# Products without a use between the first conditioning units, first norm's squares added by VectorE, down projections begun two tiles early

## The chip, the cores and the metric

One core of a Trainium2 chip runs the whole program. The metric is the device time of one execution in microseconds (us), lower is better. TensorE does the matrix products, VectorE (DVE) and ScalarE (ACT) take results out of PSUM and split operands, GpSimd (POOL) does additions beside them, and SyncE (SP) issues nearly all loads. TensorE's granted clock has two levels, 1.2 and 2.4 GHz; the profile gives it as a share of 2.4 (0.50 and 1.00).

## The reference, cut to what matters

Two blocks run one after the other on 256 tokens of width 1024 (the first block also carries 256 context tokens). All arrays are float32. What the change touches:

```python
# conditioning of a layer: 6 vectors of 1024 for each of two token sets
mod_l = (silu(c) @ w_ada + b_ada)          # w_ada: 1024 x 6144
hl = rms_norm(xl, norm_mix) * (1 + sc1_l) + sh1_l     # the first norm

# rms_norm: x * rsqrt(mean(x * x) + 1e-6) * g

# the feed-forward parts, four in all (two per block), D_FF = 2816 = 22 x 128
swiglu(h) = (silu(h @ w_g) * (h @ w_u)) @ w_d

# second block, a chunked recurrence with gates: its 64 x 64 systems
# are solved level by level; the gates are products h @ w_gate, sigmoid
```

## The kernel before, in words

**Operands.** Activations lie feature-major: 128 features on the partitions, tokens along the row. Each float32 product is made of three faster ones: weights and activations are split into a high and a low part, and `weight_tile` (L639) issues high x high, high x low and low x high. ScalarE writes the high part of a weight unit (`act_split`, L603, L612), VectorE the low part (`dve_split`, L615, L621), both ahead of TensorE by two units. A unit is at most 128 x 2048 elements, 1 MB. SyncE loads units in the order of the list UNITS into a ring of three slots (`load_unit`, L547); a slot is free when the unit that lay there is split, or, for the conditioning weights ("raw" units), multiplied (`raw_done`).

**The start.** Eight raw units hold the first 2048 columns of the conditioning weights. `pe_ada` (L1008) goes through them on TensorE: for unit x the products `ada_products` (L989: eight products of 256 columns, each with 32 stationary columns, float32, in four column groups), then the fold of unit x - 1 (`ada_fold`, L1000, four records for two products of 2 columns), which needs ScalarE's copy of that unit (`take_ada`, L1006). A unit's products also wait until the copy of the unit two before is done. Between the units stand the sums of squares of the first norm. `act_ada` (L1026) is ScalarE's side: before the copies of units 3 to 6 it squares two tiles of 128x512 each (L727) into three buffers in turn; TensorE adds each square over the partitions by a product with a matrix of ones (`pe_square_sum`, L750), which also frees its buffer. Before the copy of unit 7 ScalarE loads the table of the square root with a small root of its own (L762) and takes the root of the sum (L767). VectorE then forms the reciprocal (L781), waits for the last fold (`ada_cols`), adds the bias to the conditioning columns (L1106), forms the scales (L1109) and scales the tokens (L802), with the low parts (L794) and two weight splits between. TensorE's first product of tokens is L647. SyncE issues in this order: parameters, raw unit 0, common constants, x (2 MB, L3077), raw units 1 to 7, and then the units of the projections.

**A feed-forward part.** `pe_ffn` (L895) goes through the up tiles: for tile i the gate and up products; ScalarE applies silu (L945), VectorE multiplies (L970), writes the high part (L972) and the low part (L973) of hidden tile i and counts `h_gated`. Then it waits for all hidden tiles, and `pe_residual` (L651) runs the down projection: eight output groups m, each over all f hidden tiles k in order, one PSUM bank per group. The first feed-forward works on 512 tokens in two halves of f = 11 (phases down0_0 and down0_1), the other three on 256 tokens with f = 22: five down projections in all. In the first one GpSimd forms part of the second layer's conditioning beside it (L1080 to L1084), summed by TensorE (L1094).

**The recurrence.** `pe_rwkv` (L2458) runs four groups, each with a solve over levels (`pe_level_p`, L2351; `pe_level_u`, L2367 and L2369), values (L2380, copied by ScalarE, L2542), the solved systems (`pe_solved`, L2391 without and L2397 with the values) and a scan of four steps that begins when ScalarE has copied the solution (L2546, L2548). Into the waits between these TensorE fits pieces of the gate product (`pe_gate`, L2828: one piece is three products of 256 columns).

Of the kernel before, what the change touches and what calls it, by code (L numbers as in the profile page):

```python
# [8 lines left out]
ALU = mybir.AluOpType  # L9
# [3 lines left out]
P = 128  # L13
D = 1024
KT = D // P
# [20 lines left out]
RING = 3  # L36
# [379 lines left out]
ADDS = KT - 2  # L416
SUMS_DONE = [KT + sum(x is not None for x in SUMS[1:r + 1]) for r in range(len(SUMS))]

# [13 lines left out]
def build(nc, dram, out):  # L432
    ctx = ExitStack()
    with ctx:
# [68 lines left out]
        def K(name):  # L503
            at, n = CONST_AT[name]
            return const[:, at:at + n]
# [144 lines left out]

        def pe_residual(pe, phase, h, c0, n, kt, norm=None, order=None, first=0):  # L651


            s0, g0 = FIRST_OF_KIND[phase], FIRST_GROUP[phase]
            order = order or list(range(kt))
            for m in range(KT):
                bank = GROUPS[g0 + m][0] if first and m < 2 else pe_group(pe, g0 + m)
                for x, k in enumerate(order):
                    if first and m < 2 and x < kt - first:
                        continue  # L660
                    t = m * kt + x
                    if t % TPU == 0:
                        pe_weights(pe, s0 + t // TPU)
                    mm = weight_tile(pe, ps[:, bank, 0:n], s0 + t // TPU, t % TPU * P, P, h[:, k, 0, c0:c0 + n],
                                     h[:, k, 1, c0:c0 + n], x == 0, x == kt - 1)
                    if x == kt - 1:
                        mm.then_inc(group_done, 1)
                    elif t % TPU == TPU - 1:
                        mm.then_inc(unit_done, 1)
            if norm is not None and norm not in LATE:  # L670
                pe_square_sums(pe, norm)
# [44 lines left out]
        def act_square(act, r, m):  # L716
# [3 lines left out]
            if r and m == 0:  # L720
                act.wait_ge(norm_sum, SUMS_DONE[r - 1])
            elif m >= 3 and r == 0:
                act.wait_ge(norm_sum, m - 2)
            elif m >= 3:
                act.wait_ge(norm_add, ADDS * (SUMS[r] - 1) + m - 2)
# [6 lines left out]
        def square_at(r, m):  # L732
            return m % 3 if r == 0 else 0 if m == 0 else 1 + (m - 1) % 2

# [11 lines left out]

        def pe_square_sum(pe, m):

            pe.wait_ge(norm_sq, m + 1)
            pe.matmul(ps[:, 5, :], K("ones"), square[:, square_at(0, m), :], start=(m == 0), stop=(m == KT - 1)).then_inc(norm_sum, 1)  # L750

# [143 lines left out]
        def pe_ffn(pe, r, norm, next_norm):  # L895
            hidden, h, n, c0 = ffn_operands(r)
            for x, f in enumerate(FFN_PARTS[r]):
# [21 lines left out]
                if r == 0 and x == len(FFN_PARTS[0]) - 1:  # L919
                    pe_ada_fold(pe, ADA_UNITS + ADA_FIRST - 1)  # L920
                pe.wait_ge(h_gated, hidden_done(r, x, f))
                final = x == len(FFN_PARTS[r]) - 1
                pe_residual(pe, f"down{r}_{x}", hidden, 0, n, f, next_norm if final else None)

# [57 lines left out]

        FIRST_SUMS = 3

# [18 lines left out]
        def take_ada(act, x, bank):  # L1003

            act.wait_ge(raw_done, x + 1)
            act.activation(ada_row(x), ps[:, bank, 0:ADA_COLS], ACT.Copy).then_inc(ada_rows, 1)  # L1006

        def pe_ada(pe):  # L1008
            pe.wait_ge(cond_ready, 2)
            for x in range(ADA_FIRST + 1):  # L1010
                if x < ADA_FIRST:
# [5 lines left out]
                else:  # L1017
                    pe.wait_ge(ada_rows, x)
                    mm = ada_fold(pe, x - 1, x - 1)
                    if x == ADA_FIRST:  # L1020
                        mm.then_inc(ada_cols, 1)
                if FIRST_SUMS <= x < FIRST_SUMS + KT // 2:
                    for m in range(2):
                        pe_square_sum(pe, 2 * (x - FIRST_SUMS) + m)

        def act_ada(act):  # L1026
            for x in range(ADA_FIRST):
                if x == FIRST_SUMS:
                    act.wait_ge(x_in, 16)
                if FIRST_SUMS <= x < FIRST_SUMS + KT // 2:  # L1030
                    for m in range(2):
                        act_square(act, 0, 2 * (x - FIRST_SUMS) + m)
                if x == ADA_FIRST - 1:
                    act_root_ready(act)
                    act_root(act, 0)
                take_ada(act, x, 4 + 2 * (x % 2))
# [1421 lines left out]
        def pe_rwkv(pe):  # L2458
            for g in range(RW_GROUPS):
# [23 lines left out]
                pe_level_p(pe, g, 4)  # L2483
                pe_gate(pe, 2 * g + 1, 5, 7)
                pe_level_u(pe, g, 4)
                pe_values(pe, g)
                pe_solved(pe, g)
                pe_gate(pe, 2 * g + 1, 7, 10)
                for c in range(4):
# [527 lines left out]
        def _(dve):  # L3017
# [3 lines left out]
            dve.memset(eps_col[:, 3:4], EPS * EPS)  # L3021
            dve.memset(cond[:, :, 2:32], 0.0).then_inc(cond_ready, 1)
            for layer in range(DEPTH):
                c0, n = unit_tokens(layer, False)
# [48 lines left out]
        def _(sp):  # L3073
            sp.dma_start(par[:, :], dram["par"]).then_inc(par_in, 16)
            load_unit(sp, 0)
            sp.dma_start(const[:, 0:COMMON_N], dram["const"][:, 0:COMMON_N]).then_inc(const_in, 16)
            sp.dma_start(xT[:, :, :].rearrange("p k t -> p (k t)"), dram["x"]).then_inc(x_in, 16)  # L3077
            for u in range(1, len(UNITS)):
                if u == RAW_UNITS[ADA_FIRST - 1] + 4:
                    sp.dma_start(const[:, COMMON_N:COMMON_N + ONE_N], dram["const"][:, COMMON_N:COMMON_N + ONE_N]).then_inc(first_in, 16)  # L3080
# [121 lines left out]
```

## Time and profile before

| | us |
|---|---|
| median of 3 runs (lowest, highest) | 1990.88 (1985.06, 1994.65) |
| the profiled execution | 1997.22 |
| its span, first to last instruction | 1995.4 |
| TensorE busy | 1859.6 (93%) |
| VectorE, ScalarE, GpSimd busy | 1155.0, 769.7, 300.9 |

The mean granted clock of the profiled execution is 0.969. Busy shares overlap; what sets the time is read from the chain of waits, which follows the last instruction back to what released it. In a timeline a row gives start, duration, engine, line, operation and operands, and in brackets the idle time before it with what ended it. Durations of pipelined products overlap, so the distance of two starts says more than a duration. A float32 product leaves two records, so x4 at L750 is two products.

### The profile page before, as it was taken

How to read it: one execution, taken by the hardware profiler on the slowest of the kernel's cores; microseconds unless marked ns; L12 is line 12 of the kernel's file. 1: busy time of each engine (PE TensorE's matmuls, PEld its weight loads, DVE VectorE, ACT ScalarE, POOL GpSimd, SP SyncE). 2: the span in 40 equal slices, each digit the busy share in tenths (PEclk: the TensorE clock that was granted, in tenths of full speed). 3: DMA queues.
4: the chain of work that ended last, by engine and by line, in shares of the span. 5: the costliest groups of instructions: out<-in, count | busy, mean ns of one | idle time of the engine just before them, and what ended most of it. 6: DMA issues, size and time to landing. Idle time of an engine off the chain costs nothing.

```text
span 1995.4 us, 34393 instructions
## 1 busy us (share of the span) xinstructions
PE 1859.6 (93%) x14988; PEld 1636.1 (82%) x14988; DVE 1155.0 (58%) x1708; ACT 769.7 (39%) x1073; POOL 300.9 (15%) x264
## 2 busy tenths in 40 slices
PE   6999878999999998887999999999998999999998
PEld 3777556777888777766999999999988778899997
DVE  2744574655253327656655576555668777676654
ACT  3432562321122224455433443333454444344332
POOL 0011001799262010100000100002001111000000
PEclk9998989999999998899999999999999999999999
DMA  8254113466354212203455565553431111255552
GB/s 322 84 195 164 64 34 115 149 196 203 116 164 153 95 65 74 96 1 127 148 177 173 180 204 185 176 183 127 159 138 44 44 44 66 86 169 188 175 174 77
DMA packets 40758, 266.22 MB, mean 133 GB/s; under 512 B 4512, under 2 KB 4640, under 8 KB 13344
## 3 DMA queue, kind: packets, MB, share of 16 engines
q1 hardware_dynamic: 35712, 244.10, 35.4%
q0 software_dynamic: 4608, 16.78, 2.7%
q8 instruction: 118, 1.93, 0.4%
q10 hardware_dynamic: 288, 3.15, 0.4%
q14 instruction: 32, 0.26, 0.0%
HBM read 262.96 MB, written 1.05 MB: 132 GB/s over the span
## 4 chain that ended last, share of the span: by engine, by line
PE 76%; DVE 13%; ACT 5%; POOL 4%; issue 2%; DMA 1%; SPq 0%; ACTq 0%; DVEq 0%; POOLq 0%
PE ps L641 19%; PE ps L642 18%; PE ps L643 18%; DVE W L621 3%; PE ps L1620 2%; POOL work L1080 2%; PE ps L989 2%; ACT W L612 1%; POOL work L1081 1%; PE ps L647 1%; PE ps L1407 1%; PE ps L2351 1%; PE ps L649 1%; PE ps L648 1%; PE ps L2369 1%
## 5 line engine op out<-in xcount | busy, mean ns | idle before, releaser
L621 DVE TENSOR_TENSOR W<-ring,W 128x2048 fp32r<-128x2048 f32 (+2 forms) x194 | 442.8, 2284 | 257.1 <-ACT W L612 256.8
L612 ACT ACTIVATE W<-ring 128x2048 fp32r<-128x2048 f32 (+2 forms) x194 | 359.0, 1853 | 139.7 <-PE ps L643 130.6
L641 PE MATMUL ps<-h_lat,W 128*128 128x256 f32 x1056 | 302.0, 286 | 5.8 <-DVE h_lat L794 4.0
L642 PE MATMUL ps<-h_lat,W 128*128 128x256 f32 x1056 | 299.9, 284 | 0.0
L643 PE MATMUL ps<-h_lat,W 128*128 128x256 f32 x1056 | 299.9, 284 | 0.0
L641 PEld LDWEIGHTS ps<-h_lat,W 128*128 128x128 f32 x1056 | 203.6, 193 | 7.5 <-issue 4.6
L642 PEld LDWEIGHTS ps<-h_lat,W 128*128 128x128 f32 x1056 | 203.9, 193 | 0.3 <-issue 0.2
L643 PEld LDWEIGHTS ps<-h_lat,W 128*128 128x128 f32 x1056 | 203.8, 193 | 0.0
L745 POOL TENSOR_TENSOR work<-work 128x256 f32<-128x256 f32 (+1 forms) x42 | 41.0, 977 | 972.9 <-ACT work L727 781.8
L641 PE MATMUL ps<-hidden_lat,W 128*128 128x256 f32 x528 | 151.1, 286 | 6.3 <-DVE hidden_lat L973 6.3
L642 PE MATMUL ps<-hidden_lat,W 128*128 128x256 f32 x528 | 150.7, 286 | 0.0
L643 PE MATMUL ps<-hidden_lat,W 128*128 128x256 f32 x528 | 150.7, 285 | 0.0
L970 DVE TENSOR_TENSOR work<-work,ps 128x256 f32<-128x256 f32 (+1 forms) x88 | 42.9, 488 | 185.8 <-ACT work L945 185.7
L641 PE MATMUL ps<-h_both,W 128*128 128x512 f32 x352 | 140.7, 400 | 8.9 <-DVE h_both L794 8.9
L642 PE MATMUL ps<-h_both,W 128*128 128x512 f32 x352 | 137.8, 391 | 0.0
L643 PE MATMUL ps<-h_both,W 128*128 128x512 f32 x352 | 137.7, 391 | 0.0
L945 ACT ACTIVATE work<-ps 128x512 f32<-128x512 f32 (+1 forms) x44 | 21.6, 490 | 267.7 <-PE ps L643 267.7
L641 PEld LDWEIGHTS ps<-hidden_lat,W 128*128 128x128 f32 x528 | 102.8, 195 | 6.9 <-DVE hidden_lat L973 6.9
L643 PEld LDWEIGHTS ps<-hidden_lat,W 128*128 128x128 f32 x528 | 102.7, 195 | 0.0
L642 PEld LDWEIGHTS ps<-hidden_lat,W 128*128 128x128 f32 x528 | 102.7, 195 | 0.0
L727 ACT ACTIVATE work<-xT 128x256 f32<-128x256 f32 (+1 forms) x64 | 31.6, 496 | 172.3 <-DVE xT L688 112.4
L641 PE MATMUL ps<-h_mix,W 128*128 128x256 f32 x312 | 92.7, 297 | 5.2 <-DVE h_mix L792 3.9
(402 smaller groups left out, 4315.4 us busy)
## 6 DMA issues: line engine op xcount, KB each, us to landing
ring<-w_up_dram SPq DMA_DIRECT2D x88, 1024.0 KB, 4.9
ring<-w_down_dram SPq DMA_DIRECT2D x43, 1024.0 KB, 4.9
ring<-w_ada_dram SPq DMA_DIRECT2D x32, 1024.0 KB, 5.6
work<-w_ada_dram POOLq DMA_DIRECT2D x32, 512.0 KB, 4.1
ring<-w_rkv_dram SPq DMA_DIRECT2D x13, 1024.0 KB, 4.9
ring<-w_fm_dram SPq DMA_DIRECT2D x10, 1024.0 KB, 4.9
ring<-w_out_dram SPq DMA_DIRECT2D x8, 1024.0 KB, 4.8
ring<-w_gates_dram SPq DMA_DIRECT2D x16, 512.0 KB, 3.6
```

The lines of the kernel that those rows point to most:

```text
L612: act.activation(slots[SLOT[s]][:, 0, 0:cols], ring[:, u % RING, 0:cols], ACT.Copy).then_inc(w_high, 1)
L621: dve.tensor_tensor(slots[SLOT[s]][:, 1, 0:cols], ring[:, u % RING, 0:cols], slots[SLOT[s]][:, 0, 0:cols], ALU.subtract).then_inc(w_low, 1)
L641: pe.matmul(o, slots[SLOT[s]][:, 0, at:at + cols], high, start=first, stop=False)
L642: pe.matmul(o, slots[SLOT[s]][:, 0, at:at + cols], low, start=False, stop=False)
L643: return pe.matmul(o, slots[SLOT[s]][:, 1, at:at + cols], high, start=False, stop=final)
L727: ins = act.activation(square[:, at, 0:n], xT[:, m, c0:c0 + n], ACT.Square, scale=1.0 / 32)
L745: pool.tensor_tensor(square[:, 0, 0:n], square[:, 0, 0:n], square[:, square_at(r, m), 0:n], ALU.add).then_inc(norm_add, 1)
L945: act.activation(stage_buf[:, i % 2, 0:n], gate, ACT.Silu).then_inc(act_emptied, 1)
L970: dve.tensor_tensor(t, t, up_banks(g, n)[1], ALU.mult).then_inc(dve_emptied, 1)
L989: mm = pe.matmul(ps[32 * g:32 * g + 32, bank, 0:ADA_COLS], cond[:, k, :], w[:, k * ADA_COLS:(k + 1) * ADA_COLS], start=(k < 4), stop=(k >= ...
L1080: plink(pool.tensor_tensor(half, half, c, ALU.mult))
L1620: mm = pe.matmul(ps[:, 2 + d, 65 * tt:65 * tt + 65], pbuf[:, s, d, tt * P:(tt + 1) * P], vones[:, s, h, :], start=(s == src[0]), stop=(s = ...
```

## The change

Four edits.

1. Start, order of loads: x is issued behind raw unit 2, just before raw unit 3. ScalarE squares four tiles before the copy of unit 3 and four before the copy of unit 4, loads the root's table there too, and takes the root before the copy of unit 6. The squares use the buffers of the later norms (one that holds the sum, two in turn).
2. Start, sums: VectorE adds the squares into one tile (seven additions of 128x512), and TensorE makes one sum over the partitions, after unit 5. The counts for the later norms (`SUMS_DONE`) fall from 8 to 1 for the first norm.
3. Start, products without a use: `pe_warm` issues float32 products of the conditioning vector's tile with itself (128 stationary columns, 256 moving) into a bank that nobody reads: 3 before unit 0, then 1 after each unit but the last, and 9 after unit 2.
4. Down projections wait at first for f - 2 hidden tiles, and for all of them before tile f - 2 of the first group. And in the recurrence one of the two gate pieces ahead of the last level's update, and one of the three behind the solve, move between the values and the solve.

```diff
-SUMS_DONE = [KT + sum(x is not None for x in SUMS[1:r + 1]) for r in range(len(SUMS))]
+SUMS_DONE = [sum(x is not None for x in SUMS[:r + 1]) for r in range(len(SUMS))]
...
-        def pe_residual(pe, phase, h, c0, n, kt, norm=None, order=None, first=0):
+        def pe_residual(pe, phase, h, c0, n, kt, norm=None, order=None, first=0, late=None):
...
+                    if late is not None and (m, k) == (0, late[0]):
+                        pe.wait_ge(*late[1:])
...
-                act.wait_ge(norm_sum, m - 2)
+                act.wait_ge(first_add, m - 2)
...
-            return m % 3 if r == 0 else 0 if m == 0 else 1 + (m - 1) % 2
+            return 0 if m == 0 else 1 + (m - 1) % 2
...
-        def pe_square_sum(pe, m):
-
-            pe.wait_ge(norm_sq, m + 1)
-            pe.matmul(ps[:, 5, :], K("ones"), square[:, square_at(0, m), :], start=(m == 0), stop=(m == KT - 1)).then_inc(norm_sum, 1)
+        first_add = sem("first_add")
+
+        def dve_first_sums(dve):
+
+            for m in range(1, KT):
+                dve.wait_ge(norm_sq, m + 1)
+                if m >= 2:
+                    dve.wait_ge(first_add, m - 1)
+                dve.tensor_tensor(square[:, 0, :], square[:, 0, :], square[:, square_at(0, m), :], ALU.add).then_inc(first_add, 1)
+
+        def pe_first_sum(pe):
+
+            pe.wait_ge(first_add, KT - 1)
+            pe.matmul(ps[:, 5, :], K("ones"), square[:, 0, :], start=True, stop=True).then_inc(norm_sum, 1)
...
-                pe.wait_ge(h_gated, hidden_done(r, x, f))
+                pe.wait_ge(h_gated, hidden_done(r, x, f - 2))
                 final = x == len(FFN_PARTS[r]) - 1
-                pe_residual(pe, f"down{r}_{x}", hidden, 0, n, f, next_norm if final else None)
+                pe_residual(pe, f"down{r}_{x}", hidden, 0, n, f, next_norm if final else None,
+                            late=(f - 2, h_gated, hidden_done(r, x, f)))
...
-        FIRST_SUMS = 3
+        FIRST_SUM = 5
...
+        def pe_warm(pe, n):
+
+            for _ in range(n):
+                pe.matmul(ps[:, 0, 0:COND_N], const[:, cond_at:cond_at + P], const[:, cond_at:cond_at + COND_N], start=True, stop=True)
+
         def pe_ada(pe):
             pe.wait_ge(cond_ready, 2)
+            pe_warm(pe, 3)
...
-                if FIRST_SUMS <= x < FIRST_SUMS + KT // 2:
-                    for m in range(2):
-                        pe_square_sum(pe, 2 * (x - FIRST_SUMS) + m)
+                if x < ADA_FIRST - 1:
+                    pe_warm(pe, 9 if x == RING - 1 else 1)
+                if x == FIRST_SUM:
+                    pe_first_sum(pe)
 
         def act_ada(act):
             for x in range(ADA_FIRST):
-                if x == FIRST_SUMS:
+                if x == RING:
                     act.wait_ge(x_in, 16)
-                if FIRST_SUMS <= x < FIRST_SUMS + KT // 2:
-                    for m in range(2):
-                        act_square(act, 0, 2 * (x - FIRST_SUMS) + m)
-                if x == ADA_FIRST - 1:
+                for m in {RING: range(4), RING + 1: range(4, KT)}.get(x, ()):
+                    act_square(act, 0, m)
+                if x == RING + 1:
                     act_root_ready(act)
+                if x == FIRST_SUM + 1:
                     act_root(act, 0)
                 take_ada(act, x, 4 + 2 * (x % 2))
...
-                pe_gate(pe, 2 * g + 1, 5, 7)
+                pe_gate(pe, 2 * g + 1, 5, 6)
                 pe_level_u(pe, g, 4)
                 pe_values(pe, g)
+                pe_gate(pe, 2 * g + 1, 6, 8)
                 pe_solved(pe, g)
-                pe_gate(pe, 2 * g + 1, 7, 10)
+                pe_gate(pe, 2 * g + 1, 8, 10)
...
             dve.memset(cond[:, :, 2:32], 0.0).then_inc(cond_ready, 1)
+            dve_first_sums(dve)
...
-            sp.dma_start(xT[:, :, :].rearrange("p k t -> p (k t)"), dram["x"]).then_inc(x_in, 16)
             for u in range(1, len(UNITS)):
+                if u == RING:
+                    sp.dma_start(xT[:, :, :].rearrange("p k t -> p (k t)"), dram["x"]).then_inc(x_in, 16)
```

## Rows read from the trace of the kernel before

**Rows 1.** The page, chain that ended last: share of the span by engine.
```profile
PE 76%; DVE 13%; ACT 5%; POOL 4%; issue 2%; DMA 1%; SPq 0%; ACTq 0%; DVEq 0%; POOLq 0%
```
**Rows 2.** Timeline of TensorE, start: start us, duration, engine, line, operation, [idle before].
```profile
14.26 1.93 PE L989 MATMUL ps<-ring,const 128*32 128x256 f32 x16 [5.94 <-DMA ring<-w_ada_dram]
16.12 1.01 PE L1000 MATMUL ps<-const,work 128*128 128x2 f32 x4
...
22.61 3.76 PE L750 MATMUL ps<-work,const 128*128 128x512 f32 x4
...
28.74 1.96 PE L750 MATMUL ps<-work,const 128*128 128x512 f32 x4
...
37.35 1.07 PE L989 MATMUL ps<-ring,const 128*32 128x256 f32 x16
38.35 1.18 PE L1000 MATMUL ps<-const,work 128*128 128x2 f32 x8
45.02 0.56 PE L647 MATMUL ps<-W,h_in 128*128 128x272 f32 x1 [5.49 <-DVE h_in L794]
```
**Rows 3.** Timelines of ScalarE and VectorE, start.
```profile
3.75 0.22 ACT L2986 ACTIVATE const<-par 128x16 f32<-128x16 f32 x1 [1.72 <-DMA par<-par_dram]
...
19.34 1.14 ACT L727 ACTIVATE work<-xT 128x512 f32<-128x512 f32 x2
...
35.53 1.28 ACT L762 ACT_TABLE_LOAD   x1
...
37.46 0.69 ACT L767 ACTIVATE work<-ps,eps_col 128x512 f32<-128x512 f32 x1 [0.43 <-PE ps L750]
38.18 3.35 DVE L781 RECIPROCAL work<-work 128x512 f32<-128x512 f32 x1 [36.97 <-ACT work L767]
...
41.57 0.19 DVE L1106 TENSOR_TENSOR mod<-ps,par 128x32 f32<-128x32 f32 x1
```
**Rows 4.** DMA in 3 to 9 us.
```profile
DMA packets 378, 2.52 MB, mean 420 GB/s; under 512 B 41, under 2 KB 169, under 8 KB 177
```
**Rows 5.** Timeline of TensorE, first product of each of the five down projections.
```profile
489.94 0.80 PE L641 MATMUL ps<-hidden_both,W 128*128 128x512 f32 x1 [3.54 <-DVE hidden_both L973]
...
684.58 0.50 PE L641 MATMUL ps<-hidden_both,W 128*128 128x512 f32 x1 [2.25 <-DVE hidden_both L973]
...
1082.47 0.39 PE L641 MATMUL ps<-hidden_lat,W 128*128 128x256 f32 x1 [1.72 <-DVE hidden_lat L973]
...
1278.38 0.39 PE L641 MATMUL ps<-hidden_lat,W 128*128 128x256 f32 x1 [2.29 <-DVE hidden_lat L973]
...
1919.69 0.58 PE L641 MATMUL ps<-hidden_lat,W 128*128 128x256 f32 x1 [2.29 <-DVE hidden_lat L973]
```
**Rows 6.** Windows: stretch, length, PE, PEld, DVE, ACT, POOL busy (xcount), granted clock, DMA, GB/s.
```profile
15.00:20.00 5.00, 5.00 (x40) 2.80 (x36) 0.00 (x0) 1.32 (x4) 0.00 (x0) 1.00 1.01 419
489.94:496.00 6.06, 6.06 (x14) 4.79 (x15) 2.68 (x1) 0.00 (x0) 5.58 (x5) 0.50 0.53 155
685.00:690.00 5.00, 5.00 (x24) 4.12 (x23) 1.74 (x1) 0.00 (x0) 0.00 (x0) 1.00 0.34 105
1083.10:1086.50 3.40, 3.40 (x18) 3.40 (x18) 2.20 (x1) 0.00 (x0) 0.00 (x0) 0.51 0.36 92
1087.00:1089.00 2.00, 2.00 (x19) 2.00 (x19) 0.00 (x0) 0.00 (x0) 0.00 (x0) 1.00 0.90 365
1919.69:1922.75 3.06, 3.06 (x14) 3.06 (x15) 2.29 (x1) 0.50 (x1) 0.00 (x0) 0.50 0.39 161
```
**Rows 7.** Timeline of VectorE ahead of the second down projection.
```profile
682.65 0.69 DVE L970 TENSOR_TENSOR work<-work,ps 128x512 f32<-128x512 f32 x1 [6.78 <-ACT work L945]
```
**Rows 8.** Timeline of TensorE, end of the first group's solve.
```profile
1551.33 0.39 PE L2838 MATMUL ps<-h_mix,gates_parts 128*128 128x256 f32 x1
...
1552.23 1.15 PE L2369 MATMUL ps<-work 64*64 64x64 f32 x32
...
1555.01 1.15 PE L2397 MATMUL ps<-work 64*64 64x64 f32 x32 [0.23 <-ACT work L2542]
```

## The prediction

> **What bounds the kernel now.** I read the page's shares first (TensorE is busy 93% of the span, in the table above), then its chain of waits, of which TensorE carries 76% [rows 1], so only idle or slow time of TensorE, or time before it can start, is worth anything. The view of waits then gives the places. At the start, TensorE is fed by eight conditioning units, interleaved with the sums of squares; the timeline of TensorE there [rows 2] shows the second unit only at 14.26 us, since the 2.1 MB of x stand ahead of it in the queue, and the last fold at 39.53 (38.35 and 1.18). ScalarE's and VectorE's rows [rows 3] show what follows one another: the root at 37.46, the reciprocal 38.18 to 41.53, and at 41.57 the addition that opens the first norm's scaling. That row is the mark for the start: all behind it up to the first token product at 45.02 is a chain of VectorE, then of splits. The other places are the starts of the five down projections: TensorE stands still until the last hidden tile's low part is written [rows 5], and in three of the five the granted clock is at its lower level, 1.2 GHz (0.50 in the rows), when it resumes or soon after [rows 6]. The solve of the recurrence has a small wait of 0.23 us in each of its four groups [rows 8].
>
> **The start.** Prices from rows 2. The eight products of a unit take 1.93 us at the low clock and 1.07 at the high one (I count 1.0 between starts), a fold 0.94 and 0.54 (half of 1.18 at the end, for two folds). Four records of square sums, two products of 512 columns, take 3.76 or 1.96. A product of no use has 256 columns and the same 128 rows, so a quarter of that: 0.94 or 0.49. There are 18: 3 ahead, 9 behind the third unit, 1 behind six others. The profile's granted clock says 1.00 in 15 to 20 us [rows 6], where the durations are those of the low level; they halve between the square sums at 22.61 and those at 28.74. For this stretch I go by durations.
>
> DMA moves 0.42 MB/us without a pause [rows 4]. A unit is 1.05 MB, 2.5 us. With x (5.0 us) out of its way the second unit lands at 9.2 instead of 14.2, the third at 11.7, x at 16.7, the others at 19.2, 21.7, 24.2, 26.7, 29.2, since each slot is freed in time. TensorE at the high clock by then: third unit ends by 13, nine products of no use reach 17.5, and the fourth unit runs from 19.2 to 20.2, as soon as it lands.
>
> ScalarE squares four tiles from 16.7. A square is 0.57 to 0.62 (1.14 for two [rows 3]); the trace has no addition of two 128x512 tiles in this stretch, so I bound it: 0.69 from the nearest row of VectorE, which reads PSUM too [rows 7], above, and half of it below; I take 0.69 plus 0.05 of hand-off. Then copy of the fourth unit to 20.8, four squares held by the two buffers to 23.5, table load and dummy root 1.5 [rows 3], copy of the fifth unit at 25.4. Here is a new wait: TensorE has the sixth unit's products done at 25.2 and cannot fold the fifth until 25.5, because ScalarE's copy stands behind the squares and the table load; queued behind the fold on TensorE are the square sum and the last two units. Then fold 26.1, product of no use 26.6, one square sum of 0.98 to 27.6 (VectorE's seventh addition is done by 24.3), root to 28.4, reciprocal 3.35 to 31.8. Beside it TensorE: seventh unit 28.6, fold 29.2, product 29.7, eighth unit 30.7, two folds 31.9. So the mark falls at 31.9, not 41.57: minus 9.7 us. The reciprocal and the conditioning end together, so neither alone is worth more. What comes behind keeps its offsets: the weights of the first projection wait on the sixth and seventh unit's products, which move more than that, and so do the constants.
>
> At the low clock throughout until the nine products raise it (around 20), the fourth unit runs at 22.2 to 23.3 and is copied at 23.7, ScalarE's second batch and the table load end at 27.7, the square sum at 30.2, the reciprocal at 34.4, and the mark is 34.6, minus 7.0. If the clock rises and then falls once more between 17.5 and 24, where TensorE is busy about half the time, the last four units and the square sum run at the low prices and the mark is near 36.5, minus 5. If all of it is low, the nine end at 24.2, the square sum at 37.3, the eighth unit at 42.9 and the folds at 44.7: mark 44.8, plus 3.2.
>
> The Trainium skill (TensorE: Matmul & The Clock Gate, "What's actually happening") says the throttled state is the default and activity releases it. By that the unbroken products from 14.26 should have raised the clock soon, and products of no use would be needless; the rows show the products of 14.26 and the square sums of 22.61 both at the low prices. By the page the units are fast from the start, the sum above is the same 9.7; by the rows it needs the dense products, and 7.0 is as fair.
>
> **The down projections.** Each issues all but the last two k-tiles of its first group before the new wait. That is 9 tiles x 3 products for the two parts of 11 tiles, 20 x 3 for the others. The rows at full clock show 24 products of 512 columns in 5.00 us, 0.21 each, and 19 of 256 columns in 2.00, 0.105 each [rows 6]; both count one product cut by each edge, so 0.23 and 0.12 are nearer. That is 5.6 to 6.2 and 6.3 to 7.2 us of work, against 1.72 to 3.54 us of waiting [rows 5]; the third tile from the end was written more than a whole up unit (48 products, 5 us or more) earlier. So the wait is wholly covered and all five gaps go: 3.54 + 2.25 + 1.72 + 2.29 + 2.29 = 12.1 us. The first weights are split two units ahead, and the bank was emptied two up units ago: neither is late next. Queued behind the moved wait is only the same group. A gap that goes takes its slow stretch with it. At 0.50 TensorE has 14 products of 512 columns in 6.06 us, which at 0.23 are worth 3.2; 18 of 256 columns in 3.40 us, some 16 of them whole, worth 1.9 to 2.0; and 14 in 3.06, worth 1.7 [rows 6]. Lost: 2.8 + 1.4 + 1.4 = 5.6 us. Together 17.7 us. None of it should be given back: weight splits here wait for TensorE to free slots, GpSimd's half of the later conditioning starts anew from TensorE's own step, and the projection's end is TensorE's.
> Bounds: all of it, or, if splits rather than TensorE set the pace of the first group, only the slow stretches.
>
> **The pieces of gate product in the solve.** One piece (three products; two take 0.90, from 1551.33 to 1552.23 [rows 8]) less before the last level's update, two after the values, two instead of three before the scan. Gain at best: the four waits of 0.23 go, 0.9 us. But the two pieces now stand ahead of the solve, whose result ScalarE must copy before the scan begins: update 0.4 earlier, then 0.8 of pieces, the copy's wait of 0.23 gone, so the scan starts about 0.24 later, four times: plus 1.0. I take the loss, since the scan already starts as the copy ends.
>
> **Sum**, against the profiled execution (1997.22, of which the span is 1995.4 and 1.8 lies around it): 9.7 + 17.7 - 1.0 = 26.4, to 1970.8. It lies 6.3 over the median of the three runs, 1990.88; how often a gap meets a slow stretch is the profile's luck, three of five here, and I have no reason to think the median had fewer. So I take the same 26.4 from the median: 1964.5, forecast 1965.
>
> **The rivals.**
> *The start's clock.* Same downs, but the start gains 5 to 7 (low until the nine products, or a second fall). Time 1967 to 1970. For it: the low prices from 14.26 to beyond 22.61 [rows 2], half-busy TensorE after 17.5. Against it: the dense stretch from 4.0 (conditioning vector ready at 3.97 [rows 3]) through the first unit and on into the second, all dense. Chance 30%.
> *Down gaps turn into another wait.* The unit's split, the bank, or the last tile comes late, and the five gaps are given back within the projection; only the start and part of the slow stretches stay: 9.7 + 3 - 1 = 11.7, 1979, or 1982 if no slow stretch goes either. Against it: VectorE is idle for 6.78 us before the last tile's product of the second part [rows 7], so nothing of its own is late. 8%.
> *The change doesn't do what it says at the start*: the mark is held by ScalarE (squares, table load, copies in one queue) so that both batches and the root come as late as now, gain 0 to 3, downs as forecast: 1971 to 1974. 7%.
> *Slower.* One mechanism: the products of no use run at 1.2 GHz, do not raise the clock, and TensorE stays low behind them. Place: the start and the projections behind it. Price: 3.2 us at the mark and 0.45 us for each us of product-bound work that follows low (1.4 of 3.06 [rows 6]). It decides only if it outlasts the 12.1 us of gaps and the 10 us of the bound below, some (12.1 + 10 - 3.2) / 0.45 = 42 us of low clock (rows 6 show stretches of 3 to 6). At 60 us of it the time is 1990.9 + 3.2 - 12.1 + 27 = 2009; 2%.
>
> Forecast 53%. **How the numbers follow.** 0.5% (10 us) is about what a measurement of this kernel tells from no change. Cases by their time: the forecast, the clock rival and the third (90%) are below 1981; of the second, whose two times stand on either side of it, I put a quarter below. Faster 0.92, within 0.5% 0.06, slower 0.02. Range 1956 to 1979: below, VectorE's additions at the lower price (1), the solve's pieces at their gain (2), slow stretches in all five gaps (2 x 1.4) and some of the spread of the runs; above, the second rival's first time.
>
> **What would show it.** The mark at 31 to 33 us (34 to 37 if the clock rival holds, with unit products of 1.93 behind 20 us); the reciprocal starting at 28.4; no idle time on TensorE ahead of the five down projections and no 0.50 behind them; TensorE's idle total down by some 22 us though its busy time grows by the products of no use; the 0.23 waits in the solve gone and a wait of about 0.3 before the first scan step. Wrong would be: idle time at the twentieth k-tile, or rows of splits as new releasers within the first down group.

## The result, and the profile after

The changed kernel takes 1967.24 us (median of 4 runs, 1962.52 to 1969.29), the kernel before 1990.61 (4 runs, 1985.06 to 1994.65): a ratio of 0.9881, 95% interval 0.9851 to 0.9911. The forecast was 1965, its range 1956 to 1979. The profiled execution of after took 1967.34 us (span 1965.5), 29.9 less than that of before, where 26.4 were predicted; between the medians it is 23.4.

First the page: busy time by engine, then the chain that ended last.
```profile
PE 1848.6 (94%) x15010; PEld 1629.9 (83%) x15010; DVE 1156.8 (59%) x1715; ACT 770.1 (39%) x1073; POOL 300.6 (15%) x264
...
PE 75%; DVE 12%; POOL 5%; ACT 5%; issue 2%; DMA 2%; DVEq 0%; ACTq 0%; POOLq 0%
```
The bound is where it was [rows 1]. The span less TensorE's busy time is 116.9 us, against 135.8 before: 18.9 us of idle are gone, of 22 expected: 12.1 ahead of the down projections and 6.8 at the start. The other 11 are busy time: products that ran faster, less the 18 products of no use.

**The start.** TensorE's timeline (start, duration, operation, idle before):
```profile
3.90 2.93 PE L1025 MATMUL ps<-const 128*128 128x256 f32 x6 [3.90 <-ACT const L3008]
6.76 1.94 PE L1003 MATMUL ps<-ring,const 128*32 128x256 f32 x16
...
9.71 1.07 PE L1003 MATMUL ps<-ring,const 128*32 128x256 f32 x16
...
13.58 4.13 PE L1025 MATMUL ps<-const 128*128 128x256 f32 x18
19.48 1.07 PE L1003 MATMUL ps<-ring,const 128*32 128x256 f32 x16 [1.77 <-DMA ring<-w_ada_dram]
...
26.52 1.02 PE L763 MATMUL ps<-work,const 128*128 128x512 f32 x2
...
30.38 1.07 PE L1003 MATMUL ps<-ring,const 128*32 128x256 f32 x16 [0.35 <-DMA ring<-w_ada_dram]
31.38 1.17 PE L1014 MATMUL ps<-const,work 128*128 128x2 f32 x8
36.25 0.57 PE L647 MATMUL ps<-W,h_in 128*128 128x272 f32 x1 [3.70 <-DVE h_in L807]
```
The second unit runs at 9.71 instead of 14.26 [rows 2]; from there all units cost 1.07, so the clock is high, and they go at the pace of their loads. The first token product starts 8.8 us earlier. Behind the idle time ahead of it the clock is low again, in after as in before; the window below shows it for after.
```profile
38.00:40.00 2.00, 2.00 (x10) 2.00 (x10) 2.00 (x5) 0.24 (x1) 0.00 (x0) 0.50 1.03 430
```
VectorE and ScalarE beside the start:
```profile
18.07 2.29 DVE L758 TENSOR_TENSOR work<-work 128x512 f32<-128x512 f32 x3 [16.86 <-ACT work L730]
21.55 3.08 DVE L758 TENSOR_TENSOR work<-work 128x512 f32<-128x512 f32 x4 [1.19 <-ACT work L730]
28.30 3.35 DVE L794 RECIPROCAL work<-work 128x512 f32<-128x512 f32 x1 [3.67 <-ACT work L780]
32.66 0.19 DVE L1127 TENSOR_TENSOR mod<-ps,par 128x32 f32<-128x32 f32 x1 [1.00 <-PE ps L1014]
...
16.89 1.67 ACT L730 ACTIVATE work<-xT 128x512 f32<-128x512 f32 x3 [3.27 <-DMA xT<-x_dram]
...
27.58 0.69 ACT L780 ACTIVATE work<-ps,eps_col 128x512 f32<-128x512 f32 x1 [1.61 <-PE ps L763]
```
The mark, the addition behind the root's reciprocal, is at 32.66 instead of 41.57 [rows 3]. It waits 1.00 us for the last fold, not for the reciprocal, which is done at 31.65.

**The down projections.** The groups of TensorE by line, first of before, then of after (busy, mean ns, idle before them):
```profile
L641 PE MATMUL ps<-hidden_lat,W 128*128 128x256 f32 x528 | 151.1, 286 | 6.3 <-DVE hidden_lat L973 6.3
...
L641 PE MATMUL ps<-hidden_both,W 128*128 128x512 f32 x176 | 69.9, 397 | 5.8 <-DVE hidden_both L973 5.8
```
```profile
L641 PE MATMUL ps<-hidden_lat,W 128*128 128x256 f32 x528 | 149.4, 283 | 0.0
...
L641 PE MATMUL ps<-hidden_both,W 128*128 128x512 f32 x176 | 68.7, 390 | 0.0
```
All 12.1 us of waiting [rows 5] are gone. The first product of each of the five, in the timeline of after, has no idle time in brackets (the first, third and fifth are shown):
```profile
472.69 0.49 PE L641 MATMUL ps<-hidden_both,W 128*128 128x512 f32 x1
...
1057.52 0.28 PE L641 MATMUL ps<-hidden_lat,W 128*128 128x256 f32 x1
...
1891.17 0.28 PE L641 MATMUL ps<-hidden_lat,W 128*128 128x256 f32 x1
```
And the window behind the first of them (columns as in rows 6) is at full clock, where the same work had 0.50 before [rows 6]:
```profile
472.69:477.00 4.31, 4.31 (x21) 3.55 (x21) 3.77 (x4) 2.25 (x2) 4.08 (x3) 1.00 0.40 127
```
From the last product of the up projection to the 48th of the down projection, read at each of the five places in both timelines, it is 18.8 us less together: 12.9 in the gaps, 6.0 in the slow stretches behind them (rounded). The prediction had 12.1 + 5.6 = 17.7.

**The solve.** TensorE at the end of the first group's solve, after; the second row is the first scan step:
```profile
1526.23 1.11 PE L2418 MATMUL ps<-work 64*64 64x64 f32 x32
...
1528.58 0.34 PE L2441 MATMUL ps<-work 64*64 64x64 f32 x4 [0.34 <-ACT work L2570]
```
The wait of 0.23 [rows 8] is gone and one of 0.34 stands ahead of the scan. From the products of the last level (the row at 1521.18 in after, 1550.25 in before) to the scan it takes 7.40 us instead of 7.16, so each of four groups loses 0.24: the plus 1.0 of the prediction.

**The rest.** The start of one and the same product in both traces gives an offset that can be followed to the end. The start gives 8.8, the down projections 18.8, the solve takes 0.9 back; some 3.3 remain, which lie where nothing was changed. These are stretches at low clock that one profile has and the other has not. Here from 290 to 300 us, before and then after:
```profile
290.00:300.00 10.00, 8.67 (x31) 6.74 (x31) 5.36 (x5) 4.49 (x6) 0.00 (x0) 0.60 0.28 89
```
```profile
290.00:300.00 10.00, 10.00 (x45) 8.23 (x44) 3.96 (x5) 3.08 (x3) 1.37 (x2) 1.00 0.30 96
```
Such stretches took 4.9 us more in before up to 300 us, 0.6 more from there to the recurrence, and net 2.1 more in after within it. They explain about half of the 6.5 us by which the difference of the profiles, 29.9, exceeds that of the medians, 23.4; the profile of before lies 6.6 above its median, that of after on its own.

### The profile page after: what moved, and what is told of

The parts are those of the page before. It is cut to its first block, busy times and chain, and to the rows that moved or that the text cites. A ratio compares the mean times of both kernels' runs of the same rounds, so it can differ in the third digit from the quotient of the medians.

```text
span 1965.5 us, 34448 instructions
## 1 busy us (share of the span) xinstructions
PE 1848.6 (94%) x15010; PEld 1629.9 (83%) x15010; DVE 1156.8 (59%) x1715; ACT 770.1 (39%) x1073; POOL 300.6 (15%) x264
## 3 DMA queue, kind: packets, MB, share of 16 engines
HBM read 262.96 MB, written 1.05 MB: 134 GB/s over the span
## 4 chain that ended last, share of the span: by engine, by line
PE 75%; DVE 12%; POOL 5%; ACT 5%; issue 2%; DMA 2%; DVEq 0%; ACTq 0%; POOLq 0%
PE ps L641 18%; PE ps L643 18%; PE ps L642 18%; DVE W L621 2%; POOL work L1101 2%; PE ps L1641 2%; POOL work L1102 1%; PE ps L1003 1%; PE ps L647 1%; PE ps L1428 1%; PE ps L648 1%; PE ps L649 1%; PE ps L2372 1%; ACT W L612 1%; PE ps L2390 1%
## 5 line engine op out<-in xcount | busy, mean ns | idle before, releaser
L641 PEld LDWEIGHTS ps<-hidden_lat,W 128*128 128x128 f32 x528 | 101.4, 192 | 0.0
L642 PEld LDWEIGHTS ps<-hidden_lat,W 128*128 128x128 f32 x528 | 101.4, 192 | 0.0
L643 PEld LDWEIGHTS ps<-hidden_lat,W 128*128 128x128 f32 x528 | 101.4, 192 | 0.0
```

The lines of the kernel that those rows point to most:

```text
L641: pe.matmul(o, slots[SLOT[s]][:, 0, at:at + cols], high, start=first, stop=False)
L642: pe.matmul(o, slots[SLOT[s]][:, 0, at:at + cols], low, start=False, stop=False)
L643: return pe.matmul(o, slots[SLOT[s]][:, 1, at:at + cols], high, start=False, stop=final)
```

## The experiments

Each was timed beside the kernel before on its chip; those medians were 1989.87 (the first four), 1989.71 (the next four) and 1989.78 (the last three). All intervals are of the ratio to the kernel before.

**One: no products of no use**, all else as changed.
```
-            for _ in range(n):
+            for _ in range(0):
```


> The changed kernel without its 18 products of no use. My theory (only dense products lift the clock at the start): units and folds stay at the low prices (1.93 and 0.94 us) until the square sum and beyond; the fourth unit still runs from its landing at 19.5, but its copy comes at 21.8, the second batch of squares and the table load end at 26, the square sum at 29.7, the eighth unit's products at 34.4, the last fold at 36.2; the mark (first addition to the conditioning columns) stands at 36 to 37 against 32.66, the time at about 1971. Rival (any unbroken activity lifts it, the page's rule, or the start is bound by loads alone): the mark stays at 32.7 or comes earlier, time 1967.

1966.36 us (1966.14 to 1968.34), ratio 0.9890, 0.9871 to 0.9908: not to be told from the changed kernel, where the theory had 1971 and a mark at 36 to 37. TensorE, then VectorE, at the start:
```profile
19.14 1.93 PE L1003 MATMUL ps<-ring,const 128*32 128x256 f32 x16 [4.19 <-DMA ring<-w_ada_dram]
...
29.47 1.94 PE L1003 MATMUL ps<-ring,const 128*32 128x256 f32 x16
31.34 0.83 PE L1014 MATMUL ps<-const,work 128*128 128x2 f32 x4
32.10 1.07 PE L1003 MATMUL ps<-ring,const 128*32 128x256 f32 x16
...
34.39 0.19 DVE L1127 TENSOR_TENSOR mod<-ps,par 128x32 f32<-128x32 f32 x1 [0.74 <-PE ps L1014]
```
The clock is low from the first product until 31.8, yet the mark is only 1.7 us later than in after. Low units of 1.93 and folds of 0.94 need 2.8 us each, against 2.5 for a load, so they almost keep up: the square sum runs at 27.49, not 29.7, and the eighth unit at 32.10, not 34.4. The 18 products are worth at most these 1.7 us here, and nothing that the time shows. The Trainium skill (TensorE: Matmul & The Clock Gate, "What's actually happening") has activity release the throttle. Here it was released only at about 31.8, behind products that had followed one another without a gap since 19.14. So the direction that the Trainium skill states is borne out, but not the prediction's reading of it, by which the units are fast from the start.

**Two: the pieces of gate product as before.**
```
-                pe_gate(pe, 2 * g + 1, 5, 6)
+                pe_gate(pe, 2 * g + 1, 5, 7)
                 pe_level_u(pe, g, 4)
                 pe_values(pe, g)
-                pe_gate(pe, 2 * g + 1, 6, 8)
                 pe_solved(pe, g)
-                pe_gate(pe, 2 * g + 1, 8, 10)
+                pe_gate(pe, 2 * g + 1, 7, 10)
```


> The changed kernel with the pieces of gate product where they were. My theory: the edit costs about 0.24 us in each of the four groups, so this one gains 0.9 us (1966.3), seen as a first scan step 0.2 us nearer to the start of the same group's last level update, with the wait of 0.23 back ahead of the solve. Rival: the edit gains the four waits, then this is 0.9 us slower (1968.1).

1966.32 us (1963.27 to 1970.08), ratio 0.9888, 0.9865 to 0.9912. One us cannot be told in the time. The trace gives it back (from the last level's products to the scan it is again 7.16 us in all four groups, instead of 7.4), so the sign of this term rests on the traces alone.

**Three: the down projections wait for all tiles, as before.**
```
-                pe.wait_ge(h_gated, hidden_done(r, x, f - 2))
+                pe.wait_ge(h_gated, hidden_done(r, x, f))
-                pe_residual(..., late=(f - 2, h_gated, hidden_done(r, x, f)))
+                pe_residual(...)
```


> The changed kernel with the wait for all hidden tiles ahead of the down projections, as before. My theory: five gaps of 1.7 to 3.5 us return (12.1 us), and a slow stretch of 1.4 to 2.8 us behind two to five of them: 1982 to 1986. Rival (the rest of the pipeline makes up for the gaps, or the fall of the clock has another cause than the gaps): 1979 or less, no 0.50 behind the gaps.

1985.33 us (10 runs, 1981.71 to 1987.07), ratio 0.9978, 0.9968 to 0.9989. That is 18.1 over the changed kernel. **Four: the same edit alone, on the kernel before:**

> The kernel before with only the down projections begun early. My theory: minus 12.1 us of gaps and minus 3 to 6 us of slow stretches, 1972 to 1976. Rival (the edit's gain needs the rest of the change, or splits take the place of the gaps): 1980 or more, with idle time on TensorE within the first down group.

1973.12 us (1972.98 to 1974.84), ratio 0.9924, 0.9902 to 0.9946: 16.8 less than before. The two agree with each other and with the 17.7 predicted, and both times are in the ranges that were expected. What is left of the change, start and solve, is 4.5 in experiment three; between experiments four and two, which differ only by the start, it is 6.8. So in these medians the start is worth some 5.4 (4.5 and the solve's 0.9) to 6.8 us, less than the 9.7 predicted and the 8.9 in the profile of after. Each ratio is uncertain by 2 to 5 us, so the difference is a hint and no more.

**Five: products of no use alone, on the kernel before.**
```
         def pe_ada(pe):
             pe.wait_ge(cond_ready, 2)
+            pe_warm(pe, 3)
...
+                if x < ADA_FIRST - 1:
+                    pe_warm(pe, 9 if x == RING - 1 else 1)
```


> The kernel before with the 18 products of no use alone; loads, squares and square sums as before. My theory: they cannot help while the second unit waits for x; the clock rises sooner but the nine products stand on the way, so the mark falls at 41 to 45 us against 41.57 and the time is within 3 us of the kernel before (1990 to 1994). Rival (the clock is the whole gain at the start): mark at 37 or earlier, time 1986.

1994.69 us (10 runs, 1991.34 to 2000.18), ratio 1.0023, 1.0010 to 1.0036: slower, by a quarter of a per cent. VectorE's row:
```profile
46.19 0.19 DVE L1114 TENSOR_TENSOR mod<-ps,par 128x32 f32<-128x32 f32 x1
```
The mark is 4.6 us later than before, the time 5.0; both are just beyond what the theory allowed. In the old order TensorE has no idle time behind the second unit for them to lie in: they stand in its queue.

**Six: x loaded ahead of the second unit, as before.**
```
-                if u == RING:
+                if u == 1:
                     sp.dma_start(xT[...], dram["x"]).then_inc(x_in, 16)
```


> The changed kernel with x loaded ahead of the second unit, as before. My theory: the second unit lands at 14.2, the third at 16.7, the nine products run from 18.3 to 22.7 at the high clock or to 26.7 at the low one, and with the fourth unit so late the mark is at 35 to 39 us against 32.66: time 1970 to 1973. Rival (the order of loads is the whole gain): mark at 41, time 1975 or more. Second rival (the order is worth nothing since the total of bytes bounds the start): mark at 33, time 1967.

1971.60 us (1968.09 to 1975.73), ratio 0.9912, 0.9888 to 0.9936. TensorE, then VectorE:
```profile
14.25 1.94 PE L1003 MATMUL ps<-ring,const 128*32 128x256 f32 x16 [4.88 <-DMA ring<-w_ada_dram]
...
20.86 6.59 PE L1025 MATMUL ps<-const 128*128 128x256 f32 x18
...
39.75 0.19 DVE L1127 TENSOR_TENSOR mod<-ps,par 128x32 f32<-128x32 f32 x1 [0.19 <-PE ps L1014]
```
The second unit is back at 14.25, the dense block is low for most of its 6.59 us, and the mark is 7.1 later than in after, a little beyond the 35 to 39 expected. In the time it is 4.4. The order of loads carries most of the start's gain; without it the products of no use are again in the way. What the old order would give without them was not run.

**Seven: the gaps of experiment three filled** with products of no use ahead of the wait (7 of 256 columns at the first place, 4 elsewhere). It tells the cost of the idle time from that of the clock.
```
+                b0 = pe_group(pe, FIRST_GROUP[f"down{r}_{x}"])
+                for _ in range(7 if (r, x) == (0, 0) else 4):
+                    pe.matmul(ps[:, b0, 0:T], K("ones"), const[:, 0:T], start=True, stop=True)
                 pe.wait_ge(h_gated, hidden_done(r, x, f))
```


> As the previous one on down projections: the wait for all hidden tiles is back, but TensorE issues products of no use (7 of 256 columns ahead of the first, 4 ahead of the other four) into the bank that the first group will use. My theory: the gaps cost their 12.1 us, the clock stays at the high level behind them: 1979 to 1980, and 2 to 6 us less than the kernel with bare gaps. Rival (the falls have another cause, or products of no use do not hold the clock): 0.50 behind some of the gaps, same time as with bare gaps.

1973.83 us (1970.93 to 1978.93), ratio 0.9925, 0.9902 to 0.9949. The window behind the first down projection, experiment three and then seven:
```profile
473.28:477.00 3.72, 3.72 (x11) 2.91 (x12) 2.68 (x1) 0.00 (x0) 3.40 (x3) 0.62 0.34 99
```
```profile
471.36:476.00 4.64, 4.64 (x20) 3.86 (x21) 2.68 (x1) 0.00 (x0) 4.24 (x4) 1.00 0.50 128
```
From the last up product to the first down product it is still 4.28, 2.98, 2.00, 2.57 and 2.57 us, as in before, but the clock holds at all five places, where it fell at three of five in before and in experiment three each. So the slow stretch comes of TensorE standing still, not of the projection. The first down products now take 5.7 us (10.8 in the two parts of 512 columns) for 48, where experiment three had 12.4, 10.8, 5.7, 7.2 and 7.3. That is 4.6 us of the 11.5 between the two medians. The theory had 2 to 6 us and 1979 to 1980, so its size is missed. In the two profiles (11.1 apart) the rest can be placed by the offset of the same products: 1.9 at the start, where the mark is at 34.67 in three and 32.76 in seven, and 4.5 between 700 and 850 us, where nothing differs but three has a slow stretch at 820 to 835 us that seven has not. Whether the filled gaps have anything to do with it is open.

**Eight: one product of no use behind each unit**, not nine behind the third.
```
-                    pe_warm(pe, 9 if x == RING - 1 else 1)
+                    pe_warm(pe, 1)
```


> The changed kernel with one product of no use behind the third unit instead of nine. TensorE is then idle from 14 to 19.5 us. My theory: the clock falls in this gap and the last five units run at the low prices, mark at 35 to 37 us, time 1970 to 1971. Rival (the clock holds, the products there are not needed): mark at 32.7, time 1967.

1968.39 us (1964.45 to 1969.57), ratio 0.9892, 0.9867 to 0.9916.
```profile
19.29 1.94 PE L1003 MATMUL ps<-ring,const 128*32 128x256 f32 x16 [5.23 <-DMA ring<-w_ada_dram]
...
22.04 1.20 PE L1025 MATMUL ps<-const 128*128 128x256 f32 x2
...
37.26 0.19 DVE L1127 TENSOR_TENSOR mod<-ps,par 128x32 f32<-128x32 f32 x1 [0.47 <-PE ps L1014]
```
TensorE was fast at 11.91 (a unit in 1.07), stood still for 5.23 us, and came back low. The products of no use then cost about 1 us each in a row of units that has no slack: the mark is 2.9 later than with none. At the mark a few such products are worse than none; the times, 1968.39 and 1966.36, are within the noise of each other.

**Nine: the long wait ahead of the solve's first products filled**, with the pieces as in two.
```
                 pe_gate(pe, 2 * g, 0, 16)
+                pe.wait_ge(rw_taken, 4 * g + 4)
+                for _ in range(4 if g else 2):
+                    pe.matmul(ps[:, 7, 0:T], K("ones"), const[:, 0:T], start=True, stop=True)
                 pe_level_p(pe, g, 0)
```


> The changed kernel with the pieces of gate product where they were, and with products of no use (2 of 256 columns in the first group, 4 in the other three) in the idle time ahead of each group's first level, 1.09 and three times 2.15 us. My theory: the gate pieces give 1.0 us back, and the slow stretch of 3.4 us behind some of these idle times (1.5 us lost in each; two of four in the profile of the changed kernel) never comes: 1963 to 1965, no 0.50 between 1500 and 1700 us. Rival (the falls there come regardless, or the products run over the idle time): stretches at 0.50 stay, 1966 to 1968.

1965.64 us (1962.10 to 1966.00), ratio 0.9878, 0.9859 to 0.9898. Four such waits stand between 1500 and 1700 us; after, experiment two and the control each have a slow stretch behind two of them, experiment nine behind none. The second group, first after, then nine:
```profile
1550.00:1560.00 10.00, 7.85 (x117) 6.33 (x115) 6.01 (x6) 3.82 (x6) 6.42 (x5) 0.83 0.35 105
```
```profile
1555.00:1560.00 5.00, 4.58 (x72) 3.25 (x73) 3.01 (x4) 2.27 (x4) 4.11 (x3) 1.00 0.37 107
```
But on the same chip the changed kernel took 1963.07 (experiment eleven), so no gain can be measured, and the 1963 to 1965 expected is just missed.

**Ten: the squares summed by TensorE, tile by tile**, as before, and the root ahead of the last unit's copy; loads and products of no use as changed.
```
-            pe.wait_ge(first_add, KT - 1)
-            pe.matmul(ps[:, 5, :], K("ones"), square[:, 0, :], start=True, stop=True)
+            pe.wait_ge(norm_sq, m + 1)
+            pe.matmul(ps[:, 5, :], K("ones"), square[:, square_at(0, m), :], start=(m == 0), stop=(m == KT - 1))
```


> The changed kernel with the first norm's squares summed by TensorE tile by tile, two between the units from the fourth on, and the root ahead of the eighth unit's copy, as before; loads and products of no use as changed. My theory: each of the units four to seven is followed by 1.96 us of sums, so TensorE needs 4.0 us for each instead of the 2.5 us of its load; root at 35.5, reciprocal to 39.6: mark at 39 to 40 against 32.66, time 1973 to 1975. Rival (loads bound the start whoever adds): mark at 33 to 35, 1967 to 1969.

1971.05 us (1967.98 to 1973.10), ratio 0.9904, 0.9881 to 0.9927.
```profile
21.45 1.88 PE L763 MATMUL ps<-work,const 128*128 128x512 f32 x4
...
35.47 3.35 DVE L794 RECIPROCAL work<-work 128x512 f32<-128x512 f32 x1 [34.25 <-ACT work L780]
38.85 0.19 DVE L1128 TENSOR_TENSOR mod<-ps,par 128x32 f32<-128x32 f32 x1
```
With two sums between units a unit comes every 3.8 us, not every 2.5, and the reciprocal holds the mark at 38.85: VectorE's additions and the earlier root that they allow are together worth 6.2 us there. The time is 3.8 above the changed kernel's and 8.0 above the control's on the same chip; 1973 to 1975 was expected.

**Eleven: the changed kernel once more**, with nothing edited, as the measure for nine and ten.

> The changed kernel itself once more, on the same chip as the two before it: 1967, mark at 32.7. It tells how far its time and its slow stretches vary from run to run; stretches that start at a gap may be elsewhere in this profile.

1963.07 us (1961.10 to 1967.26), ratio 0.9872, 0.9851 to 0.9893. Its profile has another start than that of after. TensorE and VectorE, and then the windows:
```profile
25.33 1.12 PE L1003 MATMUL ps<-ring,const 128*32 128x256 f32 x16 [1.38 <-ACT work L1020]
...
28.25 1.91 PE L763 MATMUL ps<-work,const 128*128 128x512 f32 x2
30.09 1.94 PE L1003 MATMUL ps<-ring,const 128*32 128x256 f32 x16
...
37.28 0.19 DVE L1127 TENSOR_TENSOR mod<-ps,par 128x32 f32<-128x32 f32 x1 [3.01 <-PE ps L1014]
```
```profile
26.00:28.00 2.00, 2.00 (x14) 1.53 (x7) 0.00 (x0) 0.38 (x1) 0.00 (x0) 0.55 1.01 422
...
145.00:170.00 25.00, 25.00 (x168) 18.63 (x167) 11.94 (x28) 6.84 (x14) 2.71 (x6) 1.00 0.51 182
```
TensorE stands still for 1.38 us ahead of the sixth unit. The row names ScalarE's copy, but these products need the copy of the fourth unit only, done by 20.9; what came last is the unit's own load. It was issued at 13.06 in the control and 13.23 in after; size and time to landing, first control, then after:
```profile
ring<-w_ada_dram SPq DMA_DIRECT2D x1, 1024.0 KB, 12.1
```
```profile
ring<-w_ada_dram SPq DMA_DIRECT2D x1, 1024.0 KB, 11.1
```
So it lands at 25.20 instead of 24.33, and the products start 0.13 behind it in both. Then the clock falls to 0.55 although the nine products have run, and the mark comes at 37.28. This is the time of the prediction's clock rival, in the very kernel, and a late load stands ahead of it. The profiled execution still takes as long as after's (1967.26 against 1967.34), because from 145 to 170 us it has a full clock, worth 6.4 us, where after has this:
```profile
145.00:170.00 25.00, 25.00 (x129) 19.63 (x128) 8.49 (x21) 3.40 (x8) 1.79 (x4) 0.73 0.39 145
```

## Why the prediction was right

**Start, minus 9.7: right in mechanism, 0.8 too large in this profile.** The mark is at 32.66, not 31.9. The reciprocal started at 28.30 (28.4 was predicted). The missing 0.8 is in the loads. The fourth to the sixth unit land at 19.35, 21.84 and 24.33, 0.1 later than worked out, the seventh and the eighth at 27.75 and 30.24, 1.0 later. The sum had TensorE come to these two only 0.9 and 0.5 behind their landing (27.6 and 29.7), so their products are 0.3 and 0.7 late. From 24.5 to 28 us the queue is full (DMA share 1.01 at 398 GB/s) but moves 1.4 MB where a unit has 1.05. In the control the same happens one unit earlier:
```profile
DMA packets 193, 1.46 MB, mean 413 GB/s; under 512 B 16, under 2 KB 16, under 8 KB 16
```
These are the 3.5 us from the fifth landing to the sixth, 21.67 to 25.20, when nothing but the seventh and eighth unit was in the queue behind it; the weights of the first projection were issued at 26.49. So a part of the units behind moved ahead of the sixth's last piece. Why one unit falls back, and which, is open. The term mis-sized is thus the landing of the last units, and with it the conditioning, not the reciprocal, ends last. The new wait of the fifth fold behind ScalarE's copy is 0.08 us in after, and 0.84 in experiment six. One price was misread too: half of 1.18 is 0.59, not 0.54, and a fold at the high clock takes 0.47 between starts.

**The start's clock, a rival at 30%, is seen in two of six profiles.** Six have the changed start with its nine products: the mark is at 32.66, 32.68, 34.67, 32.76, 33.42 and 37.28 (after, and experiments two, three, seven, nine and eleven). In two of them the clock fell once more behind the nine: in experiment three for the last unit alone (1.94 us), in eleven from the end of the sixth unit's products on. In both a late load had kept TensorE idle just before, 1.59 us ahead of the seventh unit in three and 1.38 ahead of the sixth in eleven; the other four have at most 1.11 us behind the fourth unit. That is not a proof: the 1.7 to 1.8 us ahead of the fourth unit, right behind the nine products, were followed by a fall in none of the six. The prediction treated the loads and the clock as independent. Two profiles have the old start, with 41.57 and 40.40 (before, and four). The means, 33.9 and 41.0, are 7.1 us apart, and the medians of one chip gave 5.4 to 6.8. So what the prediction priced as one case or the other can occur within one kernel.

**Down projections, minus 17.7: right.** The sites show 18.8, the edit alone 16.8, undoing it 18.1. Its split into idle time and clock also holds at the sites (12.9 and 6.0, where 12.1 and 5.6 were predicted). Between the medians of three and seven the filled gaps count for 11.5, and of that only the 4.6 at the sites is explained.

**Solve, plus 1.0: right in the trace** (four times 0.24, from 7.16 to 7.4 in each group), beneath what the time can tell.

**The forecast for the median** took the profile's 26.4 from it and came out 2.2 below what was measured. The medians of before, four and two, all on one chip, go 16.8 and 6.8 down, together 23.6 without the solve, where the terms said 27.4: there nearly all of the difference is the start. But on the control's chip the changed kernel gains 26.7 (1989.78 to 1963.07). So the same change was measured at 23.4 and at 26.7, on either side of the 26.4, and whether the sum is too large for the median is not settled. That the time came within 2.2 us is in part luck: the stretch at 145 to 170 us, which no term has, moves 6.4 us from one execution to another, and 1967.24 is also inside the clock rival's 1967 to 1970. What carries the prediction is the places, not the total.

The rivals in which another wait takes the gaps' place, or ScalarE holds the mark for 6 us or more, did not show. Nor did the slower one, which needed some 42 us of low clock behind the start. The low clock does come back behind the start, which the prediction does not mention: behind the idle time ahead of the first token product (3.56 to 5.49 us) these products, 272 columns wide, start 0.23 us apart for 2.9 to 6.2 us and then 0.13 apart, in all thirteen profiles. In before it lasts 4.0 us and in after 4.2, so it drops out of the difference, and neither kernel has had this time removed.

## What to carry to other kernels

A wait for a whole array's last tile can move into the first group of products as far as the tiles that are ready reach; its gain is the gap and the slow products behind it, here worth nearly half of the gap once more. Dummy products can help only where the engine would stand idle: in its queue between real work they cost their own time, and if the clock is low, twice that. At this start they gained nothing that could be measured; in the gaps they kept the clock. Where a short stretch has two clock histories, sum both, since one profile shows only one of them. And where a row names a wait that had long been over, look at when the load landed.

## What the runs showed of the hardware

Granted clock is not a property of the kernel alone: in two executions (after and the control, beside medians of the kernel before that agree within 0.1%) the same kernel had the later part of its start high or low, and 145 to 170 us at 0.73 or 1.00. Idle times of 1.7 to 3.5 us ahead of the down projections were followed by the low level at three of five places in the profile of before and at three of five in that of experiment three, and by none where dummy products filled them. Idle times of 3.56 to 5.49 us ahead of the first token product were followed by it in all thirteen profiles. A load of 1.05 MB that others follow in its queue landed 2.5 us behind the one before it in most cases, and 3.4 to 4.7 behind it once in each changed start, with the queue full (in the control 1.46 MB in 3.5 us, 413 GB/s). An addition of two 128x512 tiles by VectorE took 0.69 us, the upper of the prediction's bounds, and 0.80 from one start to the next where each waits for the one before. And the rows of the clock read 1.00 in 15 to 20 us of before where the durations are those of the low level [rows 6]: for the first stretch of a kernel durations are the better witness.
